# First projections moved ahead of the last turns at three entries of a two-layer decoder trunk

## The reference

```python
h = rms_norm(x, norm_mix_g[layer])
z = h @ w_in[layer]                      # then the mixers of the layer
x = x + concat(mixer outputs) @ w_out[layer]
h = rms_norm(x, norm_mlp_g[layer])
x = x + square(relu(h @ mlp_w_up[layer])) @ mlp_w_down[layer]   # 1024 -> 4096 -> 1024
```

## Time and profile before

| what | value |
|---|---|
| runs | 2718.35 us median of 3 (2717.45 to 2719.07) |
| the profiled execution, its own time | 2719.63 us |
| its span in the profile | 2717.9 us |
| mean granted TensorE clock | 0.957 |
| TensorE busy (products) | 2502.4 us, 92% |
| GpSimd busy | 1353.7 us, 50% |
| VectorE busy | 1591.4 us, 59% |
| ScalarE busy | 1051.3 us, 39% |

### The profile page before, as it was taken

The page is one execution under the profiler, slowest core; times in us unless marked ns, Lnnn a source line. Parts: engine busy times, 40 slices in busy tenths (PEclk is TensorE's granted clock), DMA queues, the critical chain, the costliest instruction groups (busy, mean ns, idle before and its releaser), DMA issues.

```text
span 2717.9 us, 31347 instructions
## 1 busy us (share of the span) xinstructions
PE 2502.4 (92%) x11111; PEld 1989.0 (73%) x11133; DVE 1591.4 (59%) x2354; ACT 1051.3 (39%) x1741; POOL 1353.7 (50%) x770
## 2 busy tenths in 40 slices
PE   6899798789778899999999989989998999999999
PEld 4677676345677688888888877766677888888887
DVE  6478568984786554445554655656444446544472
ACT  4255587555443432223232144525443222322220
POOL 4201233887664165456665813127615566654591
PEclk9999899799899899999999999988988999999999
DMA  4211122000300211122110222102002122111211
GB/s 148 51 28 28 32 63 87 22 8 5 124 16 1 62 46 39 39 62 62 56 38 30 77 97 55 62 15 75 20 13 64 53 62 62 53 33 37 62 54 70
DMA packets 164002, 136.57 MB, mean 50 GB/s; under 512 B 22969, under 2 KB 137730, under 8 KB 163906
## 3 DMA queue, kind: packets, MB, share of 16 engines
q1 hardware_dynamic: 152658, 124.58, 15.2%
q10 hardware_dynamic: 11248, 10.75, 1.5%
HBM read 116.17 MB, written 13.63 MB: 48 GB/s over the span
## 4 chain that ended last, share of the span: by engine, by line
PE 73%; DVE 8%; issue 8%; ACT 4%; POOL 4%; DMA 0%; ACTq 0%; another core or an unknown queue 0%; DVEq 0%; POOLq 0%
PE ps L2150 22%; PE ps L2151 21%; PE ps L2152 21%; PE ps L2345 1%; ACT signs L1218 1%; POOL diag L837 1%; PE ps L2262 1%; POOL cl L892 1%; PE ps L2504 1%; DVE ub L2043 1%; PE ps L2333 1%; PE ps L2353 1%; POOL w_lo L722 1%; DVE shared L2040 1%; PE ps L2344 1%
## 5 line engine op out<-in xcount | busy, mean ns | idle before, releaser
L2150 PE MATMUL ps<-h_hi,w_hi 128*128 128x512 f32 x1680 | 673.0, 401 | 13.6 <-POOL w_lo L740 9.7
L2151 PE MATMUL ps<-h_lo,w_hi 128*128 128x512 f32 x1680 | 662.0, 394 | 0.0
L2152 PE MATMUL ps<-h_hi,w_lo 128*128 128x512 f32 x1680 | 661.5, 394 | 0.0
L2150 PEld LDWEIGHTS ps<-h_hi,w_hi 128*128 128x128 f32 x1680 | 320.4, 191 | 83.2 <-issue 14.4
L722 POOL TENSOR_TENSOR w_lo<-w_raw,w_hi 128x1024 fp32r<-128x1024 f32 x73 | 182.7, 2503 | 378.0 <-ACT w_hi L1228 375.5
L2151 PEld LDWEIGHTS ps<-h_lo,w_hi 128*128 128x128 f32 x1680 | 320.6, 191 | 68.3 <-issue 3.9
L2152 PEld LDWEIGHTS ps<-h_hi,w_lo 128*128 128x128 f32 x1680 | 319.8, 190 | 67.9
L2040 DVE TENSOR_TENSOR x_res<-ps,x_res 128x1024 f32<-128x1024 f32 x224 | 268.8, 1221 | 115.1 <-PE ps L2152 115.1
L2021 DVE TENSOR_TENSOR u_all<-ps,u_all 128x512 f32<-128x512 f32 x112 | 77.4, 691 | 416.0 <-ACT u_all L1125 416.0
L740 POOL TENSOR_TENSOR w_lo<-w_raw,w_hi 128x1024 fp32r<-128x1024 f32 x112 | 267.0, 2401 | 104.2 <-ACT w_hi L1114 104.2
L2150 PE MATMUL ps<-w_hi,uo_hi 128*128 128x512 f32 x784 | 307.6, 392 | 3.1 <-DVE shared L2040 3.1
(11 more groups left out here) (349 smaller groups left out, 4573.9 us busy)
## 6 DMA issues: line engine op xcount, KB each, us to landing
w_raw<-in_mlp_w_up SPq DMA_DIRECT2D x64, 512.0 KB, 4.1
w_raw<-in_mlp_w_down SPq DMA_DIRECT2D x64, 512.0 KB, 3.8
w_raw<-in_even_w_in SPq DMA_DIRECT2D x23, 512.0 KB, 3.7
x_res<-in_x SPq DMA_DIRECT2D x16, 512.0 KB, 8.5
w_raw<-in_odd_w_in SPq DMA_DIRECT2D x10, 512.0 KB, 3.7
scr_x<-x_res SPq DMA_DIRECT2D x8, 512.0 KB, 2.6
x_res<-scr_x SPq DMA_DIRECT2D x8, 512.0 KB, 5.0
out<-x_res SPq DMA_DIRECT2D x8, 512.0 KB, 2.6
```

Of the source, the lines that this page charges most:

```text
L2150: t_.matmul(out_, ah, bh, start=first, stop=False)
L2151: t_.matmul(out_, ah, bl, start=False, stop=False)
L2152: return t_.matmul(out_, al, bh, start=False, stop=last)
```

## The change

At all three entries the first projected half (tokens of tiles 0 to 3) is put ahead of the turn of tile 7, and of that of tile 6 in two of them. For this the halves swap their parts in the MLP scheme (`S_UP`, `quarter` and the targets in `x`), so that a pass begins with tiles 0 to 3; the first pass is written out ahead of the loop on TensorE, ScalarE, GpSimd and SyncE, with its own waits; ScalarE rounds the first two units inside the norm (`first_weights`); GpSimd's memset of `shared` moves behind the second low part; SyncE may load the first two units early; and the output projection of layer 1 puts its sums into banks 0 to 3, its waits for earlier sums moving from tile 0 to tile 2. In layer 1's mixer the first four halves are reordered (`HALVES1`), and turned tiles go to other banks.

```diff
+        HALVES1 = [(0, 0), (1, 0), (0, 1), (1, 1)] + [(n, hf) for n in range(2, len(MIX1)) for hf in range(2)]
...
-                return proj_done, H_MIX1 + 2 * (n - U_MIX1) + 2
+                return proj_done, H_MIX1 + (n - U_MIX1 + 3 if n < U_MIX1 + 2 else 2 * (n - U_MIX1) + 2)
...
-        S_UP = ((1, 1), (2, 1), (3, 1), (0, 1), (0, 0), (1, 0), (2, 0), (3, 0))
+        S_UP = ((1, 0), (2, 0), (3, 0), (0, 0), (0, 1), (1, 1), (2, 1), (3, 1))
...
-        def quarter(hf, c):
-            return u_all[:, 2 * c:2 * c + 2, hf * HT:(hf + 1) * HT]
+        def quarter(r, c):
+            return u_all[:, 2 * c:2 * c + 2, (1 - r) * HT:(2 - r) * HT]
...  SyncE
-                sp.wait_ge(down_done, mlp_base(layer)[1])
-                with sp.Fori(0, S_ITERS) as i:
+                def group(i, begins=False):
                     for r, j in enumerate((1, 2, 3, 0)):
                         sp.wait_ge(w_ready, S_UNITS * i + (first + r - 3))
+                        if begins and r == 2:
+                            sp.wait_ge(down_done, mlp_base(layer)[1])
...
+                group(0, True)
+                with sp.Fori(1, S_ITERS) as i:
+                    group(i)
...  GpSimd
-                pool.wait_ge(down_done, g0)
-                g.memset(shared[:], 0.0).then_inc(shared_zero, 1)
-                with pool.Fori(0, S_ITERS) as i:
+                def group(i, begins=False):
                     for r, j in enumerate((1, 2, 3, 0)):
                         low(i, r + 1, j, raws[r])
+                        if begins and r == 1:
+                            pool.wait_ge(down_done, g0)
+                            g.memset(shared[:], 0.0).then_inc(shared_zero, 1)
...  banks
-            return 0 if phase == 1 else 4
+            return 0 if phase % 2 else 4
         def turned_bank(phase, t, b):
+            if phase == 2:
+                return (2 * t + 2 + b) % 4 if t < 6 else 4 + (2 * t + b) % 4
             return 4 - first_bank(phase) + (2 * t + b) % 4
...  ScalarE
+            def first_weights(layer, r):
+                _, g0, n0, _, _, _ = mlp_base(layer)
+                act.wait_ge(raw_landed[r], landed_mlp[n0][r] + 16)
+                act.wait_ge(down_done, g0 if layer else g0 - 16)
+                s.activation(w_hi[:, r + 1, :], raws[r], ACT.Copy).then_inc(w_hi_ready, 1)
...  in norm(phase), for t in range(T), behind the root of tile t
                     if t >= 1:
                         high(t - 1)
+                    if phase == 1 and t >= 6:
+                        first_weights(0, t - 6)
+                    if phase == 3 and t == 7:
+                        first_weights(1, 0)
                 high(T - 1)
+                if phase == 3:
+                    first_weights(1, 1)
...  ScalarE, mixer of layer 1
-            for kind, j, _ in MIX1:
-                for hf in range(2):
+            for m, hf in HALVES1:
+                kind, j, _ = MIX1[m]
...
-                if n < U_OUT1:
+                if p % 2 == 0 and n < U_OUT1:
                     round_weights(n)
...  VectorE
-                dve.wait_ge(proj_free, H_MIX1 + 4 * j + 2)
+                dve.wait_ge(proj_free, H_MIX1 + (4 * j + 2 if j else 3))
...  TensorE: both output projections run t in range(T) only, and so leave out the turns of tiles 6 and 7
+                    for p, (j, hf) in enumerate(S_UP):
+                        if begins:
+                            if p == 0 and layer:
+                                turn(phase, 6)
+                            if p in (0, 4):
+                                pe.wait_ge(n_lo, 16 * phase + (8 if p == 0 else 16))
+                            if p < 2:
+                                pe.wait_ge(x_added, g0 - 1 + p)
                         if p < 4:
                             pe.wait_ge(w_ready, S_UNITS * i + (n0 + p + 1))
                         pe.wait_ge(proj_free, 8 * i + (h0 + p - 3))
                         project(h0 + p, j, hf)
+                        if begins and p == 0:
+                            if not layer:
+                                turn(phase, 6)
+                            turn(phase, 7)
...
+                group(0, True)
+                with pe.Fori(1, S_ITERS) as i:
+                    group(i)
...  TensorE, mixer of layer 1
-            turn(2, T - 2)
-            turn(2, T - 1)
-            pe.wait_ge(n_lo, 48)
...
+            for n, hf in HALVES1:
+                kind, j, _ = MIX1[n]
+                if (n, hf) == (0, 0):
+                    pe.wait_ge(n_lo, 32 + 10)
+                elif n == 1 and hf == 0:
+                    turn(2, T - 2)
+                    turn(2, T - 1)
+                elif n == 0:
+                    pe.wait_ge(n_lo, 48)
+                project_unit_half(p, U_MIX1 + n, hf)
```

More of the change, by code:

```diff
@@ L1171, in mlp @@
                     operand(6, ub[:])
+                act.wait_ge(down_done, g0)
+                group(0, True)
+                with act.Fori(1, S_ITERS) as i:
+                    group(i)
                 h1, u1, q1 = h0 + 8 * S_ITERS, u0 + 7 * S_ITERS, q0 + 4 * S_ITERS
@@ new lines, in _ @@
+            for m, hf in HALVES1:
+                kind, j, _ = MIX1[m]
+                src = ps[:, p % 4, :]
+                if kind == "cg":
+                    act.wait_ge(proj_done, p + 1)
+                    if j >= 2:
+                        act.wait_ge(oc_ready, j - 1)
+                    s.activation(gel[:, j % 2, hf * HT:(hf + 1) * HT], src, ACT.Gelu_apprx_tanh).then_inc(proj_free, 1)
+                    if hf == 1 and j >= 1:
+                        root(j - 1)
+                elif kind == "cx":
+                    act.wait_ge(proj_done, p + 1)
+                    if j >= 2:
+                        act.wait_ge(conv_done, j - 1)
+                    s.activation(xpad[j % 2][:, 3 + hf * HT:3 + (hf + 1) * HT], src, ACT.Copy).then_inc(proj_free, 1)
+                    if hf == 1 and j >= 1:
+                        gates(j - 1)
+                elif kind == "dv":
+                    act.wait_ge(oc_ready, 4)
+                    values_part(nv, dv[:, 4 * hf:4 * hf + 4, :], p, vtmp1[:])
+                    nv += 1
+                else:
+                    if kind == "dq" and j == 0 and hf == 0:
+                        act.wait_ge(conv_done, 4)
+                    rope_part(1, kind, j, hf, p)
+                    if kind == "dq" and j == 0 and hf == 0:
+                        gates(3)
+                    if kind == "dq" and j == 1 and hf == 1:
+                        root(3)
+                    if kind == "dk":
+                        if hf == 0:
+                            query_root(1)
+                        key_root(1, hf)
+                p += 1
@@ L2044, in mlp_by_halves @@
                 dve.wait_ge(x_added, g0 + S_SUMS * S_ITERS)
-                for rows, fs in ((slice(0, 4), 1), (slice(4, 8), 0), (slice(4, 8), 1)):
+                for rows, fs in ((slice(4, 8), 1), (slice(0, 4), 0), (slice(0, 4), 1)):
                     dst = x[:, rows, fs * HT:(fs + 1) * HT]
@@ L2187, in out_projection_of_recurrence @@
                 pe.wait_ge(hg["att_read"], 8 * T)
[L2188 to L2192, removed]
+                for t in range(T):
+                    pe.wait_ge(hg["o_lo"], t + 1)
+                    down((h_hi, h_lo), list(range(4, 8)), g0 + 2 * t, t, n0 + 8 if t == 0 else None, k0=4,
+                         bank0=first_bank(phase))
                     if t == 2:
@@ L2201, in out_projection_of_attention @@
                 pe.wait_ge(w_ready, n0 + 8)
[L2202 to L2209, removed]
+                for t in range(T):
+                    pe.wait_ge(att["o_lo"], T + t + 1)
+                    down((h_hi, h_lo), list(range(4)), g0 + 2 * t, t, k0=4, bank0=first_bank(phase))
+                    if t == 2:
+                        pe.wait_ge(x_added, g0)
+                        pe.wait_ge(att["o_copied"], 4 * T)
+                        pe.wait_ge(att["o_norm"], 2 * T)
                     if t >= 2:
@@ L2585, in _ @@
             p = H_MIX1
[L2586 to L2589, removed]
-                        follow(1, *pending)
-                    pending = (kind, j, hf, p)
-                    p += 1
-                    if hf == 1 and kind == "cx" and j >= 1:
-                        gate_products(j - 1)
-                    if hf == 0 and kind == "dq" and j == 0:
-                        gate_products(3)
-                    if kind == "dv":
-                        turn_spread_scales(1, 2 * hf)
-                        turn_spread_scales(1, 2 * hf + 1)
+            for n, hf in HALVES1:
[8 more added lines that the diff above has]
+                project_unit_half(p, U_MIX1 + n, hf)
+                if pending is not None:
+                    follow(1, *pending)
+                pending = (kind, j, hf, p)
+                p += 1
+                if hf == 1 and kind == "cx" and j >= 1:
+                    gate_products(j - 1)
```

(5 more changed lines are left out.)

47 lines of the change are left out of this document (9 added, 38 removed).

## The result

| | kernel before | changed kernel |
|---|---|---|
| median of the runs | 2717.45 us (7 runs) | 2726.15 us (7 runs) |
| lowest to highest | 2710.92 to 2719.91 | 2719.50 to 2727.07 |
| profiled execution, its own time | 2719.63 | 2719.50 |
| its span | 2717.9 | 2717.7 |

The ratio is 1.003 with a 95% interval of [1.002, 1.0039], so the change costs 8.2 us (5.4 to 10.6). The forecast was 2721.1 us, in a range of 2714 to 2727, with "within 0.2%" as the likeliest outcome and 0.23 for slower. The time lies in the range, but 5 us above the forecast, on the slower side of 0.2%, and 1 us under the top of the range.

What follows compares the result with a forecast made beforehand. TensorE was taken as the bound, so only its idle or half-speed time could be gained, at most some 39 us. A -0.6, B -2.2 and C +5.5 gave +2.7 us on 2718.35: 2721.1 us, range 2714 to 2727.

Steps and rivals of the forecast that it cites:

- The second units are late: At all three entries TensorE waits for the next unit's weights: 4.2 us at A, 6.2 at B, 5.3 at C.
- A: Entry into the MLP of layer 0; forecast -0.6 us, or -4.3 with full clock in both halves.
- C: Entry into the MLP of layer 1; forecast +5.5 us, or +3.7 with full clock in the second half.
- B: Entry into layer 1's mixer; forecast -2.2 us, or -4.0 at full clock.
- The start of the first halves: First half starts once unit 1's low part is ready: 931.2 at A, 2046.8 at C.
- The slow halves: Each half behind a new gap at the three entries takes 7.25 us, in place of 5.44 at full clock.
- slower low parts: Unknown cost: three of GpSimd's low parts on the path, beside a busy VectorE, could add up to 3.4 us; taken as none.
- loop entries: Unknown cost: entering the MLP loop in mid-stream, up to 1.75 us each, twice 3.5; taken as 0.
- Rival 1: Second units' weights are there in time at all three entries: -18.7 us, 2699.7 us; chance 0.06.
- Rival 2: Clock stays up in the new gaps at the entries: -4.6 us, 2713.8 us, or part of it; chance 0.15.
- Rival 3: New loop entries stall TensorE at pass 1's first product in both MLPs: +6.2 us, 2724.6 us; chance 0.22.
- The swap: Swapping the halves of tokens in the MLP scheme leaves a pass's operations and sizes unchanged; costed at nothing.

Runs made afterwards that it cites:

- e1: Changed kernel with the turns of tiles 6 and 7 both ahead of the first half at A and C; 2702.99 us, ratio 0.9945.
- e2: Changed kernel with ScalarE rounding both first units directly behind tile 5's high parts at A and C; 2700.28 us, ratio 0.9937.
- e3: Changed kernel with GpSimd splitting unit U_MIX1 + 1 ahead of the memset of gw at B; 2719.14 us, ratio 1.0009.
- e4: Changed kernel with products of no use in TensorE's idle time at the three entries; 2708.88 us, ratio 0.9969.
- e5: The changed kernel itself, measured once more against the kernel before; 2725.81 us, ratio 1.003.
- e6: Kernel before with only the swapped halves and the written-out first pass of both MLPs; 2718.40 us, ratio 1.0003.
- e7: Changed kernel with e2 and e3 together, and unit U_MIX1 + 4 rounded behind the copy of the third half; 2694.19 us, ratio 0.9912.
- e8: e7 with, at A, units rounded behind tiles 2 and 3 and tile 6 turned first; memset of shared moved behind the last add; 2691.28 us.

## Why the prediction was right, and what it missed

- **The second units are late.** Right at all three entries. The turns behind the first half, ScalarE's high parts, the rounding and the low part take 6.28 us at A and 6.29 at C (forecast 6.3), B's idle is 6.23 (6.2). e1, e2 and e3 each take away one cause and the waits go with it. Shown.
- **The start of the first halves.** 6.44 us after tile 5's turn began at A (6.3) and 12.38 at C (12.4). Right.
- **The first half at B** starts at once at full clock: 1607.7 to 1613.0. Right.
- **The slow halves: this term was mis-sized.** The step is "I take the slow half, 7.25". They took 8.14, 7.94, 8.17 and 7.90 us at A and C, +3.2 us in all over four halves. I took the value from one row and used it as the upper bound as well; the slow halves of B and C in the same trace took 7.42 and 7.07 us, so it had a spread that I didn't look up. Behind waits of the same length C's halves took 6.91 and 7.26 us in e3's profile, so one number was too little for this term whatever its size. With the measured halves the same sum gives +5.9, near what the profiles show (+5.6 and +6.7). e4 shows that it is the clock. Why the clock came back later isn't shown. In the kernel before, tile 7's turn ran at half speed ahead of the first half, and in the new gaps at A and C no such work stood; but a longer idle isn't the reason, since 4.37 us of idle gave 7.94 us where 4.87 had given 7.25.
- **What stays open.** The two profiles give +5.6 and +6.7 in the entries, the runs +8.2 with intervals that reach down to 5.4 and 4.9. The profiles are single executions. From tile 5's turn at A to the end of the span they last 1793.0 us before, 1797.3 and 1800.5 in the two of the changed kernel:

  | profile | against before, from tile 5's turn at A on | runs | its execution against the median of its runs |
  |---|---|---|---|
  | the change, first | +4.3 | +8.2 | -6.65 |
  | e5, the change again | +7.4 | +8.2 | -0.4 |
  | e1 | -9.8 | -14.9 | +6.0 |
  | e2 | -13.1 | -17.1 | +3.9 |
  | e3 | +1.8 | +2.4 | +1.2 |
  | e4 | -7.5 | -8.4 | -0.2 |
  | e6 | +0.5 | +0.8 | -1.8 |
  | e7 | -23.5 | -23.9 | +0.1 |
  | e8 | -30.1 | -26.4 | -4.0 |

  Where the profiled execution lies within 2 us of its median, profile and runs agree within 1 us; where it doesn't, they part in the direction in which it was off. So most of the 2 us, and of the surplus of e1 and e2 over what was expected, goes with which execution was profiled; the other executions have no trace that could show where. e4's entries stand 10.8 and 11.9 us below those of the two profiles of the change, its runs 16.6; against the second profile a further 3.2 us lie between B's end and C's turn (385.2 us against 388.4), in the mixer. Why that stretch and the one before A differ between executions is open.
- **Luck.** The forecast's own range ended at 2724, and 2726.15 lies above it. The time is inside 2714 to 2727 thanks to the room left for slower low parts (3.4 us) and loop entries (3.5 us), and neither cost anything: the low parts on the path at A and C took 2.34 and 2.35 us, and e6 shows no stall.
- **Rival 1** (the units are in time, -18.7) was not the outcome. e2 and e7 put the units in time by hand: -17.1 for A and C with B as changed, -23.9 with all three. They also start C's first half 6 us earlier, which rival 1 didn't have. **Rival 2** (clock up) is refuted: the clock read 0.50 in the first 2 us of all five halves behind a wait for weights. **Rival 3** (loop entry) is refuted by e6: it had carried the 0.22 of "slower", so the side that came out had its chance for the wrong reason. The slower side should have hung on the clock's term.
- **The swap** at nothing: right, by e6.

## What to carry to other kernels

When work is moved ahead on one engine, look up what stands behind it in the queues of the others: here three weight units (one at each entry) had landed and waited, in ScalarE's or GpSimd's queue, behind a turn which the move itself had delayed. Put work that depends on nothing (a rounding, a split) ahead of work that depends on the moved engine, and only then reorder that engine. An unbroken idle stretch of TensorE (4.4 to 9.9 us) cost its length here and 1.5 to 3.1 us more in the half behind it, so cutting one gap into two can cost more than the one gap did.

## What the runs showed of the hardware

The cost of coming back from the low clock (1.2 GHz) was 1.5 to 3.1 us for a projected half of 5.44 us behind unbroken idle, and most of that spread showed in the same place under the same order: 7.11 and 8.49 us at B behind 6.2 us of idle (the change, twice), and 8.17 and 6.91 us at C behind 9.9 (the change and e3). In e8 the granted clock was 1.00 until the first half began and had a mean of 0.76 in it, which made it 7.15 us: its first product took 0.47 us as at full clock, the third 0.63. Ahead of it stood two turns and only 0.32 and 2.22 us of idle, 4.66 us without a projection product in all. So the clock fell behind less idle than in any of the gaps of the changed kernel above, and only once the engine was at work again. With products of no use in the gaps (e4) it stayed at 1.00.
